# One decoder block on one core: attention values in eight batches, gate projections spread, level 64 in one bank, two buffers of compressed weights

## What is computed

```python
# recurrence, a head at a time: scores between two tokens carry the product of the decays between them
decay = jnp.exp(jnp.where(causal, diff, -jnp.inf))
scores = jnp.einsum('bhtd,bhsd,bhtsd->bhts', qb, kb, decay)
# attention b, a block of 128 queries at a time
s_c = jnp.einsum('bghqd,bgcd->bghqc', qb, k_cmp) * scale + bias_gh[...]   # 31 compressed keys
p_c = masked_softmax(s_c, dist_c >= 0, -1)
o_c = jnp.einsum('bghqc,bgcd->bghqd', p_c, v_cmp)
... # the same softmax over the selected keys (o_s) and over the window (o_w)
return gb[..., 0:1] * o_c + gb[..., 1:2] * o_s + gb[..., 2:3] * o_w
# merge
mixed = jax.nn.sigmoid(gate_a) * y_a + jax.nn.sigmoid(gate_b) * y_b
```

## Time and profile before

| | us |
|---|---|
| median of 3 runs | 793.69 (793.47 to 793.85) |
| profiled execution | 794.33 |
| its span, first to last instruction | 792.6 |
| TensorE busy in the span | 784.2 |
| VectorE, ScalarE, GpSimd busy | 410.4, 216.2, 489.7 |
| TensorE's granted clock | 0.999 of full speed |

### The profile page before, as it was taken

The page is one execution under the profiler, slowest core; times in us unless marked ns, Lnnn a source line. Parts: engine busy times, 40 slices in busy tenths (PEclk is TensorE's granted clock), DMA queues, the critical chain, the costliest instruction groups (busy, mean ns, idle before and its releaser), DMA issues.

```text
span 792.6 us, 12362 instructions
## 1 busy us (share of the span) xinstructions
PE 784.2 (99%) x4604; PEld 639.1 (81%) x4604; DVE 410.4 (52%) x580; ACT 216.2 (27%) x436; POOL 489.7 (62%) x325
## 2 busy tenths in 40 slices
PE   8999999999999999999999999999999999999998
PEld 6788878888777787778888888888888888888886
DVE  4795488946566565725467666660000567640000
ACT  6200754356422555733122222210000122210000
POOL 4666645677455756656666666766666667666563
PEclk9999999999999999999999999999999999999999
DMA  8244221233522011034223232232232322323320
GB/s 282 81 143 171 87 82 62 75 133 107 186 73 87 28 39 44 2 106 160 88 98 106 81 106 82 103 106 85 101 105 80 107 90 96 106 91 121 132 79 26
DMA packets 23548, 77.99 MB, mean 98 GB/s; under 512 B 2723, under 2 KB 3499, under 8 KB 23380
## 3 DMA queue, kind: packets, MB, share of 16 engines
q1 hardware_dynamic: 19964, 69.00, 25.9%
q10 hardware_dynamic: 3544, 8.44, 3.0%
HBM read 75.31 MB, written 4.21 MB: 100 GB/s over the span
## 4 chain that ended last, share of the span: by engine, by line
PE 94%; DVE 3%; DMA 1%; POOL 1%; issue 0%; SPq 0%; ACT 0%; DVEq 0%; POOLq 0%
PE bank L413 26%; PE bank L415 26%; PE bank L414 26%; PE bank L752 2%; PE bank L797 2%; PE bank L785 2%; PE bank L507 1%; PE bank L508 1%; PE bank L509 1%; DMA x<-in_xT 1%; PE bank L556 1%; POOL wsp L333 1%; PE bank L437 1%; PE bank L668 1%; DVE pc L1522 1%; DVE tot L1328 0%
## 5 line engine op out<-in xcount | busy, mean ns | idle before, releaser
L333 POOL TENSOR_TENSOR wsp<-wraw,wsp 128x1024 fp32r<-128x1024 f32 x124 | 305.8, 2466 | 10.4
L331 POOL TENSOR_SCALAR wsp<-wraw 128x1024 fp32r<-128x1024 f32 x124 | 135.9, 1096 | 237.4 <-PE bank L415 153.0
L413 PE MATMUL bank<-hhi,wsp 128*128 128x512 f32 x352 | 141.4, 402 | 1.8 <-DVE hlo L1239 1.2
L415 PE MATMUL bank<-hhi,wsp 128*128 128x512 f32 x352 | 137.3, 390 | 0.0
L414 PE MATMUL bank<-hlo,wsp 128*128 128x512 f32 x352 | 137.2, 390 | 0.0
L413 PE MATMUL bank<-ghi,wsp 128*128 128x512 f32 x256 | 100.4, 392 | 0.0
L415 PE MATMUL bank<-ghi,wsp 128*128 128x512 f32 x256 | 99.7, 390 | 0.0
L413 PE MATMUL bank<-uhi,wsp 128*128 128x512 f32 x256 | 99.7, 389 | 0.0
L414 PE MATMUL bank<-glo,wsp 128*128 128x512 f32 x256 | 99.6, 389 | 0.0
L414 PE MATMUL bank<-ulo,wsp 128*128 128x512 f32 x256 | 99.6, 389 | 0.0
L415 PE MATMUL bank<-uhi,wsp 128*128 128x512 f32 x256 | 99.6, 389 | 0.0
(11 more groups left out here) (271 smaller groups left out, 1052.9 us busy)
## 6 DMA issues: line engine op xcount, KB each, us to landing
wraw<-in_w SPq DMA_DIRECT2D x126, 512.0 KB, 3.3
bias_skewed<-bias_lines ACTq DMA_DIRECT2D x1, 2048.0 KB
bias<-bias_skewed ACTq DMA_DIRECT2D x1, 2048.0 KB, 8.9
x<-in_xT ACTq DMA_DIRECT2D x1, 2048.0 KB, 9.4
out<-x ACTq DMA_DIRECT2D x8, 256.0 KB, 2.0
x<-in_xT SPq DMA_DIRECT2D x3, 512.0 KB, 7.5
x<-in_xT SPq DMA_DIRECT2D x2, 256.0 KB, 5.0
wraw<-in_w SPq DMA_DIRECT2D x4, 128.0 KB, 8.4
```

The source lines that it names most:

```text
L331: pool.tensor_scalar(whi[:, two, :], wraw[:, raw, :], 1.0, 0.0, ALU.mult, ALU.add).then_inc(w_hi, 1)
L333: pool.tensor_tensor(wlo[:, two, :], wraw[:, raw, :], whi[:, two, :].bitcast(F32), ALU.subtract).then_inc(w_split, 1)
L413: pe.matmul(out_, wh, mh, start=first, stop=False)
L415: return pe.matmul(out_, wl, mh, start=False, stop=last)
```

## The change

- Level 64: all 16 matmuls write to bank 6, token blocks t = 0, 2 to its lower 64 partitions and t = 1, 3 to its upper 64. VectorE's two copies take one half each.
- `advance`: the products for the next level are formed behind those of keys and queries, after `decayed` is raised. One norm (qn 1) moves from behind level 32's step to behind level 64's.
- Compressed attention: two tiles `pc`. VectorE does `c_shift` and `c_weight` of block qb + 1 before it reads the projection behind which block qb is transposed; ScalarE's exponentials run a block ahead.
- Attention loop: both halves of `values(gi)` stand together in step 4 gi + 7, behind `turn(4 gi + 4)`; `pt_low` gets a second buffer, since that turn's output is copied before the values have read the old one.
- The gate projections stand at steps 2, 8, 14, 20, 26 (before 3, 7, 13, 19, 30), VectorE's reading of them at 4, 10, 16, 22, 28 (before 5, 9, 15, 21, 31), and gb7's parts are 3, 3 and 2 instead of 2, 4 and 2. GpSimd's splits of the next chunk go with them.

```diff
-GB_AFTER = {3: "gb2", 7: "gb3", 13: "gb4", 19: "gb5", 30: "gb6", 33: "gb7"}
-GATE_AT = {5: "gb2", 9: "gb3", 15: "gb4", 21: "gb5", 31: "gb6"}
-GB7_AT = {32: (0, 2), 33: (2, 6), 34: (6, 8)}
+GB_AFTER = {2: "gb2", 8: "gb3", 14: "gb4", 20: "gb5", 26: "gb6", 33: "gb7"}
+GATE_AT = {4: "gb2", 10: "gb3", 16: "gb4", 22: "gb5", 28: "gb6"}
+GB7_AT = {32: (0, 3), 33: (3, 6), 34: (6, 8)}
...
-                for pair in range(2):
-                    to = sc_bank()
-                    for h in (2 * pair, 2 * pair + 1):
-                        for t in range(ST):
-                            c = (h % 2) * 256 + t * 64
-                            last = pe.matmul(to[0:64, c:c + 64], k_dec[:, h, t * P:t * P + 64],
-                                             q_dec[:, h, t * P + 64:t * P + P], start=True, stop=True)
-                    last.then_inc(sc_done, 1)
+                to = sc_bank()
+                sc_banks[0] += 1
+                for h in range(HG):
+                    for t in range(ST):
+                        c, r0 = h * P + t // 2 * 64, t % 2 * 64
+                        last = pe.matmul(to[r0:r0 + 64, c:c + 64], k_dec[:, h, t * P:t * P + 64],
+                                         q_dec[:, h, t * P + 64:t * P + P], start=True, stop=True,
+                                         skip_group_check=True)
+                        if h == HG - 1 and t >= 2:
+                            last.then_inc(sc_done, 1)
...
-                done = t - VALUES
-                if done >= 8 and done % 8 == 1:
-                    pe.wait_ge(cv_placed, done // 8)
-                    values(done // 4, 0)
                 if LAG <= t < NT + LAG:
                     turn(t - LAG)
-                if done >= 0 and done % 2 == 0 and (done == 0 or done % 8):
-                    values(done // 4, done // 2 % 2)
+                if t >= VALUES + 2 and (t - VALUES - 2) % 4 == 0:
+                    gi = (t - VALUES - 2) // 4
+                    if gi and gi % 2 == 0:
+                        pe.wait_ge(cv_placed, gi // 2)
+                    values(gi, 0)
+                    values(gi, 1)
...
+            c_exp(0)
+            c_exp(1)
+            for qb in range(ST):
                 act.wait_ge(cpT_done, qb + 1)
...
-                if gi >= 1:
-                    act.wait_ge(pv_done[0], 2 * (gi - 1) + qb // 2 + 1)
-                to = (pt_low, pt_high)[qb // 2]
+                if gi >= 2 - qb // 2:
+                    act.wait_ge(pv_done[0], (2 * gi - 3, 2 * gi)[qb // 2])
+                to = (pt_low[gi % 2], pt_high)[qb // 2]
...
-                dve.tensor_tensor(totals(2 * m).rearrange("p (n one) -> p n one", one=1), t[:, :, 0:1], t[:, :, 1:2],
-                                  ALU.mult)
                 dve.tensor_tensor(kv[:, :, 0, :], kv[:, :, 0, :], t[:, :, 1:2].broadcast_to([P, nb, m]), ALU.mult)
                 link(dve.tensor_tensor(qv[:, :, 1, :], qv[:, :, 1, :], t[:, :, 0:1].broadcast_to([P, nb, m]),
                                        ALU.mult))
                 dve.sem_inc(decayed, 1)
+                last = dve.tensor_tensor(totals(2 * m).rearrange("p (n one) -> p n one", one=1), t[:, :, 0:1], t[:, :, 1:2],
+                                         ALU.mult)
...
+            c_shift(0)
+            c_weight(0)
             for qb in range(ST):
-                c_shift(qb)
-                c_weight(qb)
+                if qb + 1 < ST:
+                    c_shift(qb + 1)
+                    c_weight(qb + 1)
                 gate(("ga5", "ga6", "ga7", "gb0")[qb])
```

More of the change, by code:

```diff
@@ L140, in build_block @@
                    [at("kw_high", 190.5, [P, 2, S], F32R), at("kw_low", 168.5, [P, 2, S], F32R)]]
-        pt_low = at("pt_low", 186.5, [P, 2, 2, 256])
+        pt_low = [at("pt_low0", 186.5, [P, 2, 2, 256]), at("pt_low1", 160.5, [P, 2, 2, 256])]
         pt_high = at("pt_high", 178.5, [P, 2, 4, 256])
@@ L155, in build_block @@
         vc = at("vc", 176.5, [P, 2, DH])
-        pc = at("pc", 177, [P, 256])
+        pc = [at("pc0", 177, [P, 256]), at("pc1", 202.5, [P, 256])]
         pcT = [at("pcT0", 128.5, [P, S]), at("pcT1", 130.5, [P, S])]
@@ L734, in c_turn @@
                 for g in range(2):
-                    last = pe.transpose(bank[4][:, g * P:g * P + P], pc[:, g * P:g * P + P], ident[:])
+                    last = pe.transpose(bank[4][:, g * P:g * P + P], pc[qb % 2][:, g * P:g * P + P],
+                                        ident[:])
                 last.then_inc(cpT_done, 1)
@@ L790, in values @@
                 i, b = divmod(gi, 2)
-                pt = (pt_low, pt_high)[half]
+                pt = (pt_low[gi % 2], pt_high)[half]
                 for g in range(2):
@@ L1121, in _, with c_exp @@
                     act.dma_start(bias[:], skewed.rearrange("h p u -> p h u")).then_inc(bias_in, 16)
-            for qb in range(ST):
+            def c_exp(qb):
                 act.wait_ge(cs_shift, qb + 1)
                 nc_ = 8 * qb + 7
-                pcv = pc[:].rearrange("p (h c) -> p h c", h=NH)[:, :, 0:nc_]
+                pcv = pc[qb % 2][:].rearrange("p (h c) -> p h c", h=NH)[:, :, 0:nc_]
                 act.activation(pcv, pcv, ACT.Exp, scale=-1.0).then_inc(cp_ready, 1)
+            c_exp(0)
+            c_exp(1)
+            for qb in range(ST):
                 act.wait_ge(cpT_done, qb + 1)
@@ L1131, in _ @@
                 last.then_inc(cpT_copied, 1)
+                if qb + 2 < ST:
+                    c_exp(qb + 2)
             def exps(t):
@@ L1333, in advance @@
                 dve.sem_inc(decayed, 1)
+                last = dve.tensor_tensor(totals(2 * m).rearrange("p (n one) -> p n one", one=1), t[:, :, 0:1], t[:, :, 1:2],
+                                         ALU.mult)
+                if n == 5:
+                    link(last)
             def keep_near(n):
@@ L1349, in keep_64 @@
             def keep_64():
-                for pair in range(2):
-                    dve.tensor_copy(sc[0:64, 2 * pair:2 * pair + 2, 0:4, 64:P],
-                                    bank[6 + pair][0:64, :].rearrange("p (h t c) -> p h t c", h=2, t=4)
-                                    ).then_inc(sc_kept[pair], 1)
+                for odd in range(2):
+                    dve.tensor_copy(sc[0:64, :, odd:4:2, 64:P],
+                                    bank[6][64 * odd:64 * odd + 64, :].rearrange("p (h t c) -> p h t c", h=HG, t=2)
+                                    ).then_inc(sc_kept[1 - odd], 1)
             normed_n = [0]
@@ L1405, in _ @@
                 for raw_, gain in ((), (), ((ksn[:], g_ks),), ((kwn[:], g_kw),), ((qn[:, 0, :], g_q),),
-                                   ((qn[:, 1, :], g_q),), ((qn[:, 2, :], g_q), (qn[:, 3, :], g_q)))[n]:
+                                   (), ((qn[:, 1, :], g_q), (qn[:, 2, :], g_q), (qn[:, 3, :], g_q)))[n]:
                     norm(raw_, gain)
@@ L1498, in _ @@
             oa_low(HG - 1)
-            link(dve.memset(pc[:], 0.0))
+            for two in range(2):
+                link(dve.memset(pc[two][:], 0.0))
             def by_head(v):
@@ L1510, in c_shift @@
                     dve.wait_ge(bias_in, 16)
-                else:
-                    dve.wait_ge(cpT_done, qb)
-                pcv = pc[:].rearrange("p (h c) -> p h c", h=NH)[:, :, 0:nc_]
+                if qb >= 2:
+                    dve.wait_ge(cpT_done, qb - 1)
+                pcv = pc[qb % 2][:].rearrange("p (h c) -> p h c", h=NH)[:, :, 0:nc_]
                 s0 = 415 - 128 * qb
@@ L1566, in evacuate @@
                 dve.wait_ge(t_done[1], t + 1)
-                if gi >= 1:
-                    dve.wait_ge(pv_done[1], 2 * (gi - 1) + qb // 2 + 1)
-                to = (pt_low, pt_high)[qb // 2]
+                if gi >= 2 - qb // 2:
+                    dve.wait_ge(pv_done[1], (2 * gi - 3, 2 * gi)[qb // 2])
+                to = (pt_low[gi % 2], pt_high)[qb // 2]
                 c = qb % 2 * P
```

## The result

The changed kernel takes 794.98 us (median of 22 runs, 793.56 to 796.76) where the kernel before takes 793.67 (793.24 to 794.10): ratio 1.0015, 95% interval 1.0009 to 1.0021. The forecast was 793.8, and as the likeliest outcome no change within 0.2%. That holds, 0.15% slower, though the interval leaves zero out; and the time lies inside the range, 1.2 us above the number. Most of that 1.2 us goes with a loss of clock that no step of the prediction has.

What follows compares the result with a forecast made beforehand. TensorE, busy 784.2 of 792.6 us, was taken as the bound, with VectorE having little to spare in the loop. Terms -0.9 - 0.3 - 0.45 - 3.0 - 1.5 + 6.3 = +0.15 us gave a median of 793.8, range 791.6 to 795.7.

Steps and rivals of the forecast that it cites:

- The sum: Whole kernel: all savings and new holds add up to +0.15 us, so no change within 0.2%.
- Level 64 (-0.9): Recurrence, level 64: alternating column halves cut 2.01 us to 1.14, 0.9 saved; VectorE's two copies are not on the path.
- `advance` (-0.3): Recurrence, level 2: `decayed` comes one operation earlier, so the matmuls' 0.3 us hold goes whole and nothing is late next.
- Compressed attention (-0.45): Third and fourth `c_turn`: making the block one projection ahead removes holds of 0.25 and 0.21 us, 0.45 saved.
- Everything before the loop: All parts ahead of the attention loop together: 1.65 us shorter.
- The values and the old holds (-3.0 and -1.5): Attention loop: eight batches of values save 0.37 us each, 3.0 in all; old holds of 1.5 us go.
- The new holds (+6.3): Attention loop: turns wait for VectorE's evacuations, mainly in steps 3 to 7, 12 to 16 and 28 to 30, 6.3 us.
- The releaser in step 30: Held turns in the loop: evacuations by VectorE release them; the forecast is wrong if GpSimd's scaling does.
- rival 1: Attention loop: VectorE keeps up, new holds are 3.0 us instead of 6.3, kernel 790.6 us; chance 0.2.
- rival 2: Attention loop: the batch saves only its leaving, 1.2 to 2.0 us instead of 3.0; with 1.2, 795.6 us; chance 0.14.
- rival 3: Recurrence, level 64: its halves run one behind the other, the 0.9 us gain is lost, 794.7 us; chance 0.1.
- The rule on packing: Attention loop: packing speeds TensorE but not copying out of PSUM, which may become the bound; speaks against the new order.

Runs made afterwards that it cites:

- the lower group: Runs of the changed kernel at a granted TensorE clock of 0.999 or 1.000 over the whole span: eight of 22, 794.0 us in the middle.
- the upper group: Runs of the changed kernel at a granted TensorE clock of 0.997 or 0.998 over the whole span: fourteen of 22, 795.2 us in the middle.
- the last run above: Changed kernel with gb2 to gb6 behind steps 3, 6, 13, 21, 29, read in 5, 7, 14, 22, 30, and level 128 on bank 7 first: 788.66 us.
- the kernel with a hold of 3.66 us: Changed kernel with VectorE's copy ending `out_low` made three times over in step 28, to lengthen step 30's hold: 797.14 us.

## Why the prediction was right, and where it wasn't

**The whole.** The sum, +0.15 us, and the lower group, +0.3, agree to 0.2 us. Part of that is luck: level 64 brought 0.1 of its 0.9 us, and the loop lost 0.5 us less than forecast. The forecast of 793.8 is below the median because the median lies in the upper group.

**Level 64 (-0.9): the step that failed.** The size of the level was right, 1.13 us against 1.14 forecast. "Neither is on the path" was wrong: VectorE's products and the copy behind them, not the 5 us of projection, set the start of level 128. The trace of before had it, though no wait was named:

```profile
140.66 2.69 DVE L1362 SCALAR_TENSOR_TENSOR qn<-qn,small,rstd 128x512 f32<-128x512 f32 x1
...
146.20 1.28 DVE L1351 COPY sc<-bank 64x512 f32<-64x512 f32 x2
```

```profile
147.03 2.02 PE L593 MATMUL bank<-q_dec,k_dec 128*128 128x128 f32 x16
```

The first of the two copies (together 1.28 us) starts at 146.20, and level 128 starts right behind its end. Ahead of the copies stand the products, and ahead of these a norm of 2.69 us that lasts beyond level 64's end, so VectorE doesn't wait for level 64 at all: alone, its 0.88 us buys nothing, also where level 128 waits for one copy only (6.96 us, before 6.94). What I missed besides is in the diff: the second copy reads the same bank, so the next level waits for one copy more, +0.7 (7.68 us).

In the changed kernel the norm stands behind, and VectorE does wait for level 64:

```profile
140.77 2.58 DVE L1337 TENSOR_TENSOR k_dec<-k_dec,tot 128x1024 f32<-128x1024 f32 x1 [0.59 <-PE bank L582]
```

So there the level's length counts. The products end 4.95 us behind its first matmul, where they took 5.97 before; of this 1.0 us the second copy takes 0.7 and the small products for the next level, now ahead of the copies, 0.2. With bank 7 first, the copy's part comes back (6.11 us). No run has the norm moved and level 64 as it was, so how the 1.0 us divides between the two is not measured.

**`advance` (-0.3): right.** Level 2 starts 0.62 us earlier (102.98, 103.60), 0.29 of which stems from the kernel's first microseconds: 0.33. That "nothing is late next" was right for level 2. The norm that moved behind level 64's copies costs nothing, as forecast; that it also clears the way for the products of level 128 the prediction did not see.

**Compressed attention (-0.45): right,** 17.66 to 17.14 us: 0.5.

**Everything before the loop** was to be 1.65 us shorter; it is 1.34 in the trace, 0.29 of it from the kernel's start, and 0.85 in the median of the run without the loop's part.

**The values and the old holds (-3.0 and -1.5): together 0.6 too small.** The loop became 1.33 us longer although its new holds come to 6.4 (next paragraph), so 5.1 us stand against them, where 4.5 were forecast. The difference isn't in the batch. Its 2.32 us was exact, and in the last run above a full four steps take 7.51 us (275.55 to 283.06) with 0.19 of holding at the turn of block 0, against 7.66 in the earlier trace rows: without holds 0.34 is saved where 0.37 was forecast. It is in the old holds, which were taken from idle times and four examples. Counted from start to start, as the new ones, they come to some 2.1 in the trace of before: 1.1 at the held turn, 0.4 at the scores of step 3 and six of 0.06 to 0.15. The last run agrees: its loop takes 92.14 us (254.29 to 346.43) with some 1.3 of holds left, against 95.58 (254.93 to 350.51) without the loop's part, so 3.4 + 1.3 = 4.7 us are the batch and the old holds.

**The new holds (+6.3): right in place and in sum.** Each is the time from a group's start to the next, less what the same group takes where nothing holds it: steps 3 to 7 1.9 us (forecast 1.9; the longest named one stands at the turn of step 6, not of step 7), step 14 1.1 (1.0), step 18 with the turn of block 0 behind it 0.75 (0.75), steps 28 to 30 2.3 (2.15), and two turns of block 0 0.4 (0.5): 6.4. All but one of those with a named wait are released by VectorE's evacuation. So the step-by-step account was right; where the loop came out 0.5 us better than the forecast +1.8, it is by the old holds. But not all of the 6.4 is due to the new tables: up to the first batch, without the projections, the best tables still need 8.1 us where the changed kernel needs 9.1 (254.29 to 273.24 less two of 5.43; 255.24 to 269.73 less one), so of the 1.9 only 1.0 goes. Over the whole loop the best tables save 4.7 us (92.14 against 96.85).

**The releaser in step 30.** The prediction called itself wrong if holds were released by GpSimd's scaling. The largest is: the wait of 2.0 us is put down to `p_ring L376`. The chain after shows why that doesn't overturn the account:

```profile
333.68 0.42 DVE pt_low L1586
334.11 0.61 DVE oblo L1591
...
334.81 0.70 DVE bank L1596
335.50 0.60 DVE gates_b L1262
...
336.36 0.42 DVE p_ring L1565
...
337.06 0.88 POOL p_ring L376 x2
...
337.99 0.63 PE bank L788 x4
```

`out_low` and the reading of gb6 stand one behind the other on VectorE, 334.11 to 336.1. Behind them come both the evacuation (337.29 to 337.84) and, by way of one `shift` and the reciprocal, GpSimd's scaling (337.06 to 337.93); the two end within 0.1 us. The cause is the pile on VectorE, as forecast, and the run that takes the reading away shows it: 0.88 is left, released by the evacuation.

**The rivals.** VectorE doesn't keep up (rival 1): the holds are 6.4 us, not 3.0. The leaving isn't all that the batch saves (rival 2): four steps without holds are 0.34 us shorter, not 0.15. Level 64's halves run side by side (rival 3).

**The rule on packing.** I put the Trainium skill (TensorEngine Tiling (Array Packing), PSUM Bottleneck) beside the loop: packing speeds up TensorE and not the copying out of PSUM. The change packs nothing there that wasn't packed before. It belongs beside the level that is newly packed, and there the trace agrees in part: level 64 is 0.88 us shorter, and the two copies behind it, 1.28 us before and 1.41 after, are not. But of what holds level 128 only the second copy, 0.7 us, is copying out of PSUM; the rest is VectorE's products.

**The clock: not in the prediction at all.** The median is 1.2 us above the forecast, and 14 of 22 runs show a lower clock. Shown: every run of the kernel with a hold of 3.66 us lost some, and its trace has the fall behind the hold. Shown too: the kernels whose longest hold in the loop is 2.0 us have an upper group (14 of 22, 5 of 11, 3 of 10), and none of the nine other kernels, whose holds there are 1.2 us or less, has a single run below 0.999 (75 runs). Only argued: that in those 22 runs the fall was behind step 30. A hold of 1.7 us goes with no second group: all kernels have one at L482, at their start, and the kernel with level 64 alone has one of 1.71 at level 128.

## What to carry to other kernels

Before an instruction group is made faster, look up what its next user waits for, also where no wait is named: here a VectorE copy ended right ahead of that user's start, and VectorE itself did not wait for the faster group, so 0.88 us brought nothing, and a bank shared by two readers made it a loss of 0.7. When work is moved together into a batch, what stood beside the scattered pieces loses its cover; move it under the batch or a projection in the same change (here 790.2 us against 794 to 795 for the same arithmetic by the tables alone, 788.7 with the banks of level 128 swapped as well). And look at the granted clock of every run, not only at the profiled one: here the kernels with a hold of 2.0 us took another 1.2 to 1.6 us in half of their runs.

## What the runs showed of the hardware

TensorE's granted clock can fall after it has stood still and has started again: in the run with the longer hold it stood for 3.66 us, went on at full clock for about 0.7 us, and then was at 0.50 for some 3.4 us, which cost 1.44 us. The kernels with a hold of 2.0 us lost clock in 22 of their 43 runs; where in the span, no trace shows.

Level 64 as 32 records on alternating halves of the columns takes 1.13 us, 35 ns a record, against 63 ns one behind the other.
